# Mixture-of-experts stage: row numbers and row transfers rearranged, the last expert written out behind the loops

## What is computed

```python
def moe_ffn(h, router_w, router_b, w_gate_up, b_gate_up, w_down, b_down):
    logits = (xt @ router_w + router_b).astype(jnp.float32)
    top_v, top_i = lax.top_k(logits, TOP_K)        
    gates = jax.nn.softmax(top_v, axis=-1)
    ...
    def expert_block(args):
        idx, e = args
        xb = xpad[idx]
        gu = xb @ w_gate_up[e] + b_gate_up[e]
        x_glu = jnp.minimum(gu[:, ::2], SWIGLU_LIMIT)
        x_lin = jnp.clip(gu[:, 1::2], -SWIGLU_LIMIT, SWIGLU_LIMIT)
        act = x_glu * jax.nn.sigmoid(SWIGLU_ALPHA * x_glu) * (x_lin + 1.0)
        return act @ w_down[e] + b_down[e]
```

## Time and profile before

| what | value |
|---|---|
| median of 3 runs | 2606.51 us |
| profiled execution: span of its instructions | 2602.5 us |
| profiled execution beside the median | 4.0 us of the median lie around that span |
| TensorE busy | 2430.7 us, 93% |
| VectorE, ScalarE, GpSimd busy | 1115.6, 824.6, 146.0 us |
| DMA queue of SP (q1) | 685.19 MB, 71.1% of 16 engines' span |
| software queue of GpSimd (q0) | 8.37 MB, 9360 packets |
| expert stage, first to last item's output | 278.99 to 1233.43 us |

### The profile page before, as it was taken

How to read it: one execution, slowest core, us unless ns; L and a number is a source line. 1 busy time by engine, 2 the same in 40 slices (tenths; PEclk the granted TensorE clock), 3 DMA queues, 4 the chain that set the end, 5 groups by cost and what they waited for, 6 DMA issues and landing times.

```text
span 2602.5 us, 31931 instructions
## 1 busy us (share of the span) xinstructions
PE 2430.7 (93%) x10874; PEld 1503.4 (58%) x10874; DVE 1115.6 (43%) x1605; ACT 824.6 (32%) x1227; POOL 146.0 (6%) x210
## 2 busy tenths in 40 slices
PE   8999999999988888888999998999999999999999
PEld 4756333333322222222688776777887887777787
DVE  4566111010111111111555677756556556876554
ACT  2322211111111111111444345343444444345443
POOL 0001100010100010000000000000000000100000
PEclk9999999999999999999999999999999999999999
DMA  8768999999999999998556552445555555434554
GB/s 311 270 211 312 411 420 419 421 405 413 406 421 421 421 416 411 407 411 354 174 185 205 168 165 97 162 146 170 186 187 173 188 185 194 150 105 162 170 185 146
DMA packets 263342, 700.36 MB, mean 269 GB/s; under 512 B 29379, under 2 KB 128107, under 8 KB 213536
## 3 DMA queue, kind: packets, MB, share of 16 engines
q1 hardware_dynamic: 249780, 685.19, 71.1%
q0 software_dynamic: 9360, 8.37, 1.0%
q10 hardware_dynamic: 4124, 5.77, 0.6%
HBM read 706.05 MB, written 23.63 MB: 280 GB/s over the span
## 4 chain that ended last, share of the span: by engine, by line
PE 41%; DVE 6%; ACT 2%; issue 2%; DMA 1%; POOL 0%; SPq 0%; POOLq 0%; DVEq 0%; ACTq 0%
PE bank L709 10%; PE bank L711 9%; PE bank L710 9%; PE bank L1313 3%; PE bank L1312 3%; PE bank L1311 3%; PE bank L859 1%; PE bank L801 1%; DVE w_lo L1456 1%; PE bank L1301 1%; PE bank L883 1%; PE bank L783 1%; DVE X L1712 0%; POOL st_out L2826 0%; DVE HTl L1507 0%
## 5 line engine op out<-in xcount | busy, mean ns | idle before, releaser
L1456 DVE TENSOR_TENSOR w_lo<-raw,w_hi 128x1024 fp32r<-128x1024 f32 (+3 forms) x405 | 488.7, 1216 | 342.4 <-ACT w_hi L2464 338.2
L2464 ACT ACTIVATE w_hi<-raw 128x1024 fp32r<-128x1024 f32 (+3 forms) x405 | 426.1, 1057 | 480.3 <-PE bank L711 281.1
L709 PE MATMUL bank<-w_hi,HTh 128*128 128x512 f32 (+1 forms) x1288 | 513.3, 399 | 13.2 <-DVE HTl L1507 8.0
L711 PE MATMUL bank<-w_hi,HTl 128*128 128x512 f32 (+1 forms) x1288 | 503.1, 391 | 0.0
L710 PE MATMUL bank<-w_lo,HTh 128*128 128x512 f32 (+1 forms) x1288 | 502.9, 390 | 0.0
L709 PEld LDWEIGHTS bank<-w_hi,HTh 128*128 128x128 f32 x1288 | 244.3, 190 | 66.5 <-DVE HTl L1507 12.5
L1159 PE MATMUL bank<-W_F,HT_F 128*64 128x512 f32 (+1 forms) x512 | 248.8, 603 | 34.9 <-DMA W_F<-in_moe_w 34.9
L2144 DVE TENSOR_SCALAR arena<-bank 64x512 f32<-64x512 f32 (+1 forms) x64 | 44.3, 693 | 548.9 <-PE bank L1160 548.9
L711 PEld LDWEIGHTS bank<-w_hi,HTl 128*128 128x128 f32 x1288 | 244.3, 190 | 51.9
L710 PEld LDWEIGHTS bank<-w_lo,HTh 128*128 128x128 f32 x1288 | 244.9, 190 | 46.7
L1160 PE MATMUL bank<-W_F,HT_F 128*64 128x512 f32 (+1 forms) x512 | 248.9, 603 | 0.0
(11 more groups left out here) (439 smaller groups left out, 3401.8 us busy)
## 6 DMA issues: line engine op xcount, KB each, us to landing
W_F<-in_moe_w SPq DMA_DIRECT2D x128, 1024.0 KB, 27.2
raw<-in_moe_w SPq DMA_DIRECT2D x64, 1024.0 KB
arena<-in_moe_w SPq DMA_DIRECT2D x64, 1024.0 KB, 26.9
raw<-in_ffn_w SPq DMA_DIRECT2D x248, 256.0 KB, 2.9
raw<-in_ffn_w_gu SPq DMA_DIRECT2D x164, 256.0 KB, 3.0
raw<-in_w_in SPq DMA_DIRECT2D x76, 512.0 KB, 4.8
MIX<-in_moe_w SPq DMA_DIRECT2D x32, 1024.0 KB, 25.1
HT_F<-in_moe_w SPq DMA_DIRECT2D x32, 1024.0 KB
```

The lines of the kernel that those rows point to most:

```text
L709: pe.matmul(acc, xh, wh, start=start, stop=False)
L711: return pe.matmul(acc, xl, wh, start=False, stop=stop)
L1456: dve.tensor_tensor(lo_at(n, c), raw_at(n, c), hi_at(n, c).bitcast(F32), ALU.subtract).then_inc(lo_done, 1)
L2464: act.activation(hi_at(n, c), raw_at(n, c), ACT.Copy).then_inc(hi_done, 1)
```

## The change

1. **Ranks spread.** `RANK_OF` is the ramp 0..127 reordered: partition 64h + 4e + s holds rank 64h + 16s + e. An expert's 16 first tokens lie in partitions 0, 4, 8, ..., 60, the next 16 in 1, 5, 9, ..., and so on; `FIRST_PICK` does the same for item 0.
2. **Row transfers of 64.** Each gather and each scatter is issued as two indirect DMAs of 64 row numbers, partitions 0 to 63 and 64 to 127. The numbers of the upper half are copied to lower partitions first (`ROW_IN_ABOVE`, `ROW_OUT_ABOVE`, `ABOVE_IN`, `ABOVE_OUT`). `m_rows` and `m_out` count 32 per item.
3. **Last item out of the loops.** The loops end before it (`n_last`), and it is written out once for each engine, so that other work stands between its parts: on VectorE `pair_sum(0)` between the two activations, `pair_sum(1)` and three `w_lo` splits behind them; on ScalarE two `w_hi` splits before `take_glu(last, 1)`.
4. **Loads.** SP issues `f1`'s four tiles first, as soon as the last item has used `raw`, then the pair rows, now to `MIX`, `XE`, `AFT_F32`, `arena` and `BROWS_OF` (`PAIR_LOADS`).
5. **Sums.** Both halves' sums are formed on VectorE (`pair_sum`); `DIAG` and its 16 matmul rows (L1238) go. TensorE's `b_down` products stand inside the last item (`down_bias`), into banks 2 to 5. `X` is updated by one instruction per half with the square root factored in, after a product with `gate2`.

```diff
 MOST_RUNS = 15
...
+        RANK_OF = PT[:, 0, 0:P]
...
+        ABOVE_IN, ABOVE_OUT = (QT[0:FEW, 7, 204 + i:205 + i].bitcast(U32) for i in range(2))
+        ROW_IN_ABOVE, ROW_OUT_ABOVE = (QT[0:FEW, 6, 96 * i:96 * i + N_COLS].bitcast(U32) for i in range(2))
...
+        PAIR_ROWS = [MIX[:, 0, :], MIX[:, 1, :], XE, AFT_F32[:, :, :].rearrange("p a b -> p (a b)"),
+                     arena_at(0, D), arena_at(D, D), BROWS_OF[:, 0:D], BROWS_OF[:, D:2 * D]]
+        PAIR_LOADS = [(0, 2, MIX), (2, 1, XE), (3, 1, AFT_F32), (4, 2, arena_at(0, 2 * D)), (6, 2, BROWS_OF[:, :])]
+        PAIR_LANDED = [i for i, (a, n, place) in enumerate(PAIR_LOADS) for _ in range(n)]
+        SUM0, SUM1 = PAIR_ROWS[0], PAIR_ROWS[TOP_K]
...
+                        if t == 15 and not last:
+                            pe.wait_ge(m_rows, it * 32 + 32)
                         if between is not None:
                             between(k)
...
-                turn_rows_in(following, 0)
-                if following < P:
-                    turn_rows_in(following, 1)
+                if last:
+                    pe.wait_ge(E("b_down"), 16)
+                    down_bias(it, 0)
+                else:
+                    turn_rows_in(following, 0)
+                    if following < P:
+                        turn_rows_in(following, 1)
...
+                if last:
+                    down_bias(it, 1)
...
+            def down_bias(it, tt):
+                pe.wait_ge(m_glu_read, it * 2 + tt + 3)
+                pe.wait_ge(m_lin_read, it * 2 + tt + 3)
+                for n in range(2):
+                    pe.matmul(last_sum(tt, n), GATET[:, tt * P:(tt + 1) * P], BDOWN[:, 512 * n:512 * (n + 1)], start=True, stop=False)
...
-            with pe.Fori(n_runs * (RUN + 1) + 1, n_items) as it:
+            with pe.Fori(n_runs * (RUN + 1) + 1, n_last) as it:
                 expert(it, FEW, FEW)
...
+            expert(n_last, FEW, None, last=True)
+            pe.wait_ge(E("last_pick"), 1)
+            pe.wait_ge(m_down_read, n_last * 2 + 4)
...
+                    mm = pe.matmul(last_sum(tt, n), LAST_PICK[:, tt, :], OUTE[:, 512 * n:512 * (n + 1)], start=False, stop=True)
                 mm.then_inc(E("moe_over"), 1)
...
-                if name == "f3":
+                if name in ("f1", "f3"):
                     clear_banks()
...
+            step(dve.tensor_copy(RANK_OF.rearrange("p (h e s) -> p h e s", h=2, s=RANK_STEP),
+                                 tab("ramp").rearrange("p (h s e) -> p h e s", h=2, s=RANK_STEP)))
...
+                ins = dve.tensor_scalar(FIRST_PICK[:, tt, :].rearrange("p (e s) -> p e s", s=RANK_STEP),
+                                        tab("ramp")[:, 1:1 + FEW].rearrange("p (s e) -> p e s", s=RANK_STEP),
+                                        FIRST_AT[:, tt:tt + 1], None, ALU.is_equal)
...
-                dve.tensor_tensor(PAIR_ROW[:, i, :], tab("ramp").unsqueeze(1).to_broadcast([P, TOP_K, CAP]),
+                dve.tensor_tensor(PAIR_ROW[:, i, :], RANK_OF.unsqueeze(1).to_broadcast([P, TOP_K, CAP]),
...
-            mark(dve.tensor_scalar(ROW_IN, ROW_OUT, 2, None, ALU.logical_shift_right), "row_numbers")
+            step(dve.tensor_scalar(ROW_IN, ROW_OUT, 2, None, ALU.logical_shift_right))
+            step(dve.tensor_copy(ROW_OUT_ABOVE, ROW_OUT[FEW:P, :]))
+            mark(dve.tensor_copy(ROW_IN_ABOVE, ROW_IN[FEW:P, :]), "row_numbers")
...
+            def pair_sum(tt):
+                for j in range(TOP_K):
+                    dve.wait_ge(E(f"piece_in{PAIR_LANDED[TOP_K * tt + j]}"), 32)
+                    o, g, to = PAIR_ROWS[TOP_K * tt + j], GATE_P[:, tt, j:j + 1], (SUM0, SUM1)[tt]
+                    if j == 0:
+                        step(dve.tensor_scalar(to, o, g, None, ALU.mult))
+                    else:
+                        step(dve.scalar_tensor_tensor(to, o, g, to, ALU.mult, ALU.add))
...
+            def last_rows_added(tt):
...
+                dve.wait_ge(E("moe_over"), tt + 1)
+                s = (SUM0, SUM1)[tt]
+                for n in range(2):
+                    c = slice(512 * n, 512 * (n + 1))
+                    ins = dve.tensor_tensor(s[:, c], s[:, c], bank[2 + 2 * tt + n][:, :], ALU.add)
+                step(ins)
+                ask(tt)
...
-            for j in range(TOP_K):
-                dve.wait_ge(E(f"piece_in{j // 2}"), 32)
-                o, g = pair_row(j)
-                if j == 0:
...
-            for i in range(1 + TT):
-                ask(i)
-            split_to(FFN["f1"].n0 + 2)
+            take_linear(last, 0, FEW)
+            activate(last, 0, FEW)
+            pair_sum(0)
+            take_linear(last, 1, FEW)
+            activate(last, 1, FEW)
+            split_to(n1 + 1)
+            pair_sum(1)
+            split_to(n1 + 2)
+            out_half(last, FEW)
+            split_to(n1 + 3)
+            last_rows_added(0)
+            signal("moe_sum")
+            step(dve.tensor_tensor(PAIR_ROWS[1], SUM0, gate2, ALU.mult))
             k = rsqrt(stat(), 1.0 / D, 1e-6)
-            split_to(FFN["f1"].n0 + 3)
-            step(dve.scalar_tensor_tensor(SUM0, SUM0, rooted(k), gate2, ALU.mult, ALU.mult))
-            step(dve.tensor_tensor(X[:, 0, :], X[:, 0, :], SUM0, ALU.add))
+            last_rows_added(1)
+            step(dve.scalar_tensor_tensor(X[:, 0, :], PAIR_ROWS[1], rooted(k), X[:, 0, :], ALU.mult, ALU.add))
             signal("x1")
+            step(dve.tensor_tensor(PAIR_ROWS[TOP_K + 1], SUM1, gate2, ALU.mult))
+            k = rsqrt(stat(), 1.0 / D, 1e-6)
             rows_half(0)
-            sums = [stat(), stat()]
-            step(dve.tensor_tensor(SUMS[:, 1, 0:1], sums[0], sums[1], ALU.add))
-            k = rsqrt(SUMS[:, 1, 0:1], 1.0 / D, 1e-6)
-            for n in range(2):
-                c = slice(512 * n, 512 * (n + 1))
-                ins = dve.scalar_tensor_tensor(SUM1[:, c], bank[n][:, :], rooted(k), gate2[:, c], ALU.mult, ALU.mult)
-            step(ins)
-            signal("moe_sum")
-            step(dve.tensor_tensor(X[:, 1, :], X[:, 1, :], SUM1, ALU.add))
+            split_to(n1 + 4)
+            step(dve.scalar_tensor_tensor(X[:, 1, :], PAIR_ROWS[TOP_K + 1], rooted(k), X[:, 1, :], ALU.mult, ALU.add))
             signal("x1")
-            split_to(FFN["f1"].n0 + 4)
             rows_half(1)
 
...
-            for j in range(TOP_K):
-                if j == TOP_K - 1:
-                    act.wait_ge(m_down_read, n_items * 2 + 2)
-                ins = act.activation(DIAG[:, j, :], ident, ACT.Copy, scale=GATE_P[:, 1, j:j + 1])
-            ins.then_inc(E("last_out"), 2)
-            split_to(FFN["f1"].n0 + 4)
-            row_sum(SUM0, ACT.Square)
-            act.wait_ge(E("moe_over"), TT)
-            for n in range(2):
-                row_sum(bank[n][:, :], ACT.Square)
+            last, n1 = n_last, FFN["f1"].n0
+            take_glu(last, 0, FEW)
+            gated(last, 0, FEW)
+            act_taken(last, 0, FEW)
+            act.wait_ge(m_used, moe_used(last, 9))
+            split_to(n1 + 2)
+            take_glu(last, 1, FEW)
+            gated(last, 1, FEW)
+            split_to(n1 + 3)
+            act_taken(last, 1, FEW)
+            split_to(n1 + 4)
+            out_half(last, FEW)
+            for s in (SUM0, SUM1):
+                row_sum(s, ACT.Square)
...
-                pool.tensor_copy(NOW_IN, ROW_IN[:, col]).then_inc(m_now, 1)
-                pool.wait_ge(m_now, done)
+                pool.tensor_copy(NOW_IN[0:FEW, :], ROW_IN[0:FEW, col]).then_inc(m_now, 1)
+                pool.tensor_copy(ABOVE_IN, ROW_IN_ABOVE[:, col]).then_inc(m_now, 1)
+                pool.wait_ge(m_now, done * 2)
                 pool.sem_inc(E("moe_row_numbers_set"), 1)
-                pool.indirect_dma_start(XE, None, h_dram.ap(), bass.IndirectOffsetOnAxis(ap=NOW_IN, axis=0),
-                                        bounds_check=S - 1, oob_is_err=False).then_inc(m_rows, 16)
+                for half, now in ((slice(0, FEW), NOW_IN[0:FEW, :]), (slice(FEW, P), ABOVE_IN)):
+                    pool.indirect_dma_start(XE[half, :], None, h_dram.ap(), bass.IndirectOffsetOnAxis(ap=now, axis=0),
+                                            bounds_check=S - 1, oob_is_err=False).then_inc(m_rows, 16)
...
-            pool.wait_ge(m_rows, n_items * 16 + 16)
+            pool.wait_ge(m_down_read, n_last * 2 + 2)
+            rows_out(bass.ds(n_last, 1), n_last * 2 + 2)
+            pool.wait_ge(m_rows, n_last * 32 + 32)
...
-                    sp.wait_ge(m_out, n_items * 16)
+                    load_ffn(FFN["f1"], True, lambda i: sp.wait_ge(m_used, n_last * MOE_TILES + MOE_TILES + 4 + (FFN["f1"].n0 + i) % RAW // 2 * 2))
+                    sp.wait_ge(m_out, n_last * 32 + 32)
                     sp.sem_inc(E("rows_over"), 1)
-                    for tt in range(TT):
-                        for pair in range(2):
-                            slot = PAIRS_IN[2 * tt + pair]
```

(19 more changed lines are left out.)

86 lines of the change are left out of this document (30 added, 56 removed).

## The result

The changed kernel takes 2625.19 us (median of 4 executions, 2621.75 to 2629.97); beside it the kernel before takes 2607.27 us (median of 4). The ratio is 1.0077, with a 95% interval of [1.0061, 1.0093]: slower by some 0.8%, 18 us. The prediction was 2593.0 us, range 2580 to 2607.5.

What follows compares the result with a forecast made beforehand. The prediction took the expert stage to be bound by weight loads, with row transfers unevenly loading DMA engines. From 2606.5 us, 22 us gained in the loop and 8.5 us lost in the tail gave 2593.0 us, range 2580 to 2607.5.

Steps and rivals of the forecast that it cites:

- Diagnosis of the loop: Expert loop: weights bound the items, and item time beyond the 30.5 us of bytes belongs to unevenly placed row transfers.
- If rows load all 16 engines alike, items run at 30.5 us: Expert loop: spread ranks and transfers of 64 level the DMA engines; 22 us gained, between 0 and 32.
- At 655.24 a CAP item has just let all slots fill, so four items at 25.5: Loop behind item 12: a 21 us weight lead, used up by 5 us an item, lets four items run at 25.5 us.
- The doubled issues cost nothing: Row transfers in the loop: a second issue and one more copy use 2 of 15 us of slack, costing nothing.
- The stop at step 19: Last item: TensorE idles about 18 us until VectorE's second activation, behind `pair_sum(0)`; with the tail's other terms 8.5 us lost.
- the moved bank clearing: Tail: clearing of banks moves from between `f1`'s first matmuls to before them, 0.5 us taken back.
- If the clock stays low throughout: Tail after TensorE's idleness: far bound of the loss, 12 us, where the forecast took 2 us for the low clock.
- the 4 us that I had named: Tail: the prediction called itself wrong if the tail differed by more than 4 us from its forecast.
- Rival 1: Loop half levelled: transfers of 64 use the same eight engines; about 9 us gained, 2606.5 us with the tail; chance 0.14.
- Rival 3: Tail without the stop: pair rows land before the second activation is due; 11 us gained, 2573 us; chance 0.13 with partial form.
- Rival 2: Loop not levelled and gains nothing, TensorE's stop in the last item remains: 2615 us, slower; chance 0.07.

Runs made afterwards that it cites:

- e6: Kernel before with all row numbers out of range, so row transfers move nothing, and pair loads reading weights instead of pair rows: 2575.22 us, one execution.
- e12: Kernel before with ranks spread, gathers one transfer of 64 for items of FEW, scatters still transfers of 128: 2607.98 us, ratio 1.0009.
- e3: Kernel before with ranks spread alone, row transfers of 128 as before: 2601.51 us, ratio 0.9986.
- e1: Kernel before with the row part of the change alone, ranks spread and each row transfer as two of 64: 2616.77 us, ratio 1.0044.
- e5: Kernel before with ranks spread and one transfer per direction and item, of 64 for FEW items, of 128 for CAP items: 2607.50 us, ratio 1.0009.
- e9: Kernel before with ranks spread, gathers one transfer of 128, scatters one transfer of 64 behind items of FEW: 2595.53 us, ratio 0.9972.

## Why the prediction was wrong

**Diagnosis of the loop: right.** Rows beyond their bytes make the items long: 29.98 us without rows (e6) and 31.42 with them.

**"If rows load all 16 engines alike, items run at 30.5 us": wrong, and the main error.** The term was - 22 us; the loop gave + 6.0. The step failed twice. First, it took for granted that a row's packet costs the same (0.15 us) whichever engine brings it to whichever partition. In gathers of 64 with 14 rows and more the packets cost 168 to 234 ns, and weights' packets beside them slow down as well; with spread ranks the gather of 64 alone costs the loop 10.4 us (e12 against e3). I had weighed how many engines a transfer of 64 uses and not what they write to. Second, the condition "load all 16 engines alike" was not met. The spread in steps of four answers the steps that a transfer of 128 shows, and I carried it over to a transfer of 64 without a row: the share before the last weights is 0.91 with the split alone, 0.77 with both (e1) and 0.70 in the changed kernel. By themselves the split shortens the loop by 0.8 us and the spread by 6.6; together they lengthen it by 6.1, of which 4.1 go with the second transfers and the CAP gathers by 64 (e1 against e5). Where the step holds best, with scatters of 64 and gathers of 128 (e9), the loop gains 10.2 us, half of the 22, and the item comes to 30.96 us, not 30.4.

**"At 655.24 a CAP item has just let all slots fill, so four items at 25.5": wrong in the changed kernel.** It had 25.5, 25.3, 26.6 and then 32.0. The four came with no rows at all (e6: 25.5, 25.3, 25.3, 25.3); in e9 the fourth was 30.6.

**"The doubled issues cost nothing": not shown.** e5 halves the number of transfers against e1 and keeps the slow packets and nearly the items (31.34 against 31.41), but its loop is 4.1 us shorter. That can be the second transfers or the CAP gathers by 64.

**The stop at step 19: right in its mechanism, short in one term.** `pair_sum(0)` begins at T + 8.0 (predicted 7.9) and ends at + 12.7 (12.6), the activation ends at + 14.3 (14.0). From there the term was too small: f1 at + 37.0, not + 33.7, a loss of 12.3 us and not 8.5. Steps 19 to 23 and the bias took 11.4 us where I had 7.0 and 2 for the clock. Behind 17.8 us of idleness the granted clock was 0.60 over all of 1251.5 to 1263.5: 0.50 up to 1260.5, the lower of its two levels (1.2 GHz), and 1.00 from 1261.2; so the low clock cost 4.4 us, and not 2. (The row of L1246 has the pick products of both halves, 3.67 us; the first half's additions start 2.0 us into it, as I had it.) Some 0.9 us more lie in small gaps along the way, and the 0.5 us of the moved bank clearing were not seen. "If the clock stays low throughout" had been my far bound, 12 us, and the loss came out beside it. The term is 3.8 us off, just inside the 4 us that I had named.

**Rivals.** Rival 1's premise, that a transfer of 64 uses the same eight engines, is refuted by the 8 to 14 row packets in flight at once. Rival 3 fell with the stop. Rival 2 named the outcome's shape (the loop gains nothing, the stop decides, 2615 us) at a chance of 0.07. The result lies 10 us beyond even it, because no rival held a loop that loses, and because its stop, too, was priced at 8.5 us.

**What I should have bounded.** The trace before held no gather of 64 numbers, so its price a row was unknown on both sides. I gave it one value, 0.15 us, from transfers of 128, and let only the number of engines vary. With the lower end of the loop's term at 0, the range ended at 2607.5, and the loop's 6 us of loss and the tail's 12.3 both lay outside what it could hold.

## What to carry to other kernels

Levelling a DMA over more engines pays only if the far side takes it: ask of each direction which partitions it writes, and compare the rate (GB/s) at an equal busy share. Try two edits that aim at the same imbalance one by one: here each alone helped or did no harm, and together they lost. Of the forms tried, splitting paid in the scatter alone. And an engine that waits for a late load must have every instruction that another engine needs ahead of that wait: `pair_sum(0)` before an activation cost 11 us, and reordering instruction groups on VectorE and ScalarE took it back.
